# A two-layer hybrid decoder: the second mixer's projection in the 512-column form, with its evacuation, exponentials, transposes and norms re-ordered

## The reference

```python
for i in range(2):
    u = rmsnorm(h, norm_mix_g[i])
    m = rglru_mixer(u, ...) if i == 0 else ssd_mixer(u, ...)
    h = h + m
    h = h + swiglu(rmsnorm(h, norm_ffn_g[i]), ...)
    h = h + sigmoid(rmsnorm(h, norm_ple_g[i]) @ ple_w_gate[i]) * (p[i] @ ple_w_proj[i])
return rmsnorm(h, final_norm_g)

def ssd_mixer(u, ...):
    z, xbc, dt = split(u @ w_in)              # 4096, 6144 and 64 columns
    xbc = silu(causal_dwconv(xbc, conv_w, conv_b))
    x, B, C = split(xbc)                      # 64 heads of 64; 8 groups x state 128
    # chunks of 128 tokens: scores = (C B^T) * exp(segsum(A dt)); y = scores @ (x dt) + state terms
    y = ssd_scan(x, softplus(dt + dt_bias), -exp(a_log), B, C) + d_skip * x
    y = y * silu(z)
    y = y * rsqrt(mean(y*y over each group of 512) + eps) * norm_g
    return y @ w_out
```

## Time and profile before

| | |
|---|---|
| time, median of 3 runs | 2684.93 us (2684.62 to 2686.05) |
| the profiled execution's own time | 2686.58 us |
| its span, first to last instruction | 2684.9 us |
| mean granted PE clock | 0.998 |
| PE, DVE, ACT, POOL busy | 99%, 74%, 52%, 11% of the span |
| loads | 498.88 MB read, 187 GB/s over the span |

### The profile page before, as it was taken

The page is one execution under the profiler, slowest core; times in us unless marked ns, Lnnn a source line. Parts: engine busy times, 40 slices in busy tenths (PEclk is TensorE's granted clock), DMA queues, the critical chain, the costliest instruction groups (busy, mean ns, idle before and its releaser), DMA issues.

```text
span 2684.9 us, 47929 instructions
## 1 busy us (share of the span) xinstructions
PE 2660.2 (99%) x16895; PEld 2399.2 (89%) x16895; DVE 1993.9 (74%) x2782; ACT 1394.8 (52%) x1924; POOL 282.4 (11%) x314
## 2 busy tenths in 40 slices
PE   8999999999999999999999999999999999999998
PEld 8999888888888888899998999988888888888887
DVE  7788776665666678888896788978666556667776
ACT  6776444444444445556764567644444444444454
POOL 1001300000000111100001000032000000001211
PEclk9999999999999999999999999999999999999999
DMA  6545555556655566555555555555555665555564
GB/s 217 180 169 191 180 196 189 190 173 188 204 190 190 194 189 198 188 175 189 182 187 187 197 181 184 188 186 189 191 189 173 188 204 191 189 189 175 188 202 138
DMA packets 157054, 502.54 MB, mean 187 GB/s; under 512 B 16848, under 2 KB 25360, under 8 KB 156816
## 3 DMA queue, kind: packets, MB, share of 16 engines
q1 hardware_dynamic: 156864, 501.04, 57.3%
q10 hardware_dynamic: 80, 0.07, 0.0%
HBM read 498.88 MB, written 2.16 MB: 187 GB/s over the span
## 4 chain that ended last, share of the span: by engine, by line
PE 89%; DVE 5%; ACT 3%; issue 1%; DMA 1%; SPq 0%; DVEq 0%; ACTq 0%
PE bank L408 51%; PE bank L410 26%; PE bank L390 4%; PE bank L392 4%; PE bank L391 4%; DVE wlo L904 2%; ACT whi L615 1%; DMA wraw<-in_A 1%; DVE arena L1114 1%; PE bank L576 0%; ACT L691 0%; DVE R L1005 0%; ACT arena L691 0%; ACT arena L700 0%; PE bank L580 0%
## 5 line engine op out<-in xcount | busy, mean ns | idle before, releaser
L408 PE MATMUL bank<-R,whi 128*128 128x512 f32 x5984 | 2084.9, 393 | 0.2 <-DVE wlo L904 0.2
L410 PE MATMUL bank<-R,wlo 128*128 128x256 f32 x5984 | 1674.1, 280 | 0.0
L904 DVE TENSOR_TENSOR wlo<-wraw,whi 128x1024 fp32r<-128x1024 f32 (+2 forms) x1008 | 1164.0, 1161 | 560.2 <-ACT whi L615 558.9
L615 ACT ACTIVATE whi<-wraw 128x1024 fp32r<-128x1024 f32 (+2 forms) x1008 | 984.1, 983 | 891.4 <-PE bank L410 794.1
L408 PEld LDWEIGHTS bank<-R,whi 128*128 128x128 f32 x5984 | 1120.4, 187 | 251.6 <-DVE wlo L904 0.6
L410 PEld LDWEIGHTS bank<-R,wlo 128*128 128x128 f32 x5984 | 1130.0, 189 | 0.1
L390 PE MATMUL bank<-R,whi 128*128 128x256 f32 x1376 | 392.9, 286 | 6.4 <-DVE wlo L904 5.3
L392 PE MATMUL bank<-R,wlo 128*128 128x256 f32 x1376 | 389.6, 283 | 0.0
L391 PE MATMUL bank<-R,whi 128*128 128x256 f32 x1376 | 389.3, 283 | 0.0
L390 PEld LDWEIGHTS bank<-R,whi 128*128 128x128 f32 x1376 | 262.4, 191 | 10.9 <-DVE wlo L904 6.7
L391 PEld LDWEIGHTS bank<-R,whi 128*128 128x128 f32 x1376 | 262.5, 191 | 0.2
(11 more groups left out here) (173 smaller groups left out, 1314.9 us busy)
## 6 DMA issues: line engine op xcount, KB each, us to landing
wraw<-in_F SPq DMA_DIRECT2D x352, 512.0 KB, 3.3
wraw<-in_B SPq DMA_DIRECT2D x224, 512.0 KB, 3.3
wraw<-in_A SPq DMA_DIRECT2D x96, 512.0 KB, 3.6
wraw<-in_F SPq DMA_DIRECT2D x128, 384.0 KB, 3.1
wraw<-in_F SPq DMA_DIRECT2D x128, 320.0 KB, 3.2
wraw<-in_PL SPq DMA_DIRECT2D x64, 512.0 KB, 3.7
arena<-cs_rows SPq DMA_DIRECT2D x8, 1024.0 KB, 6.4
arena<-in_gates SPq DMA_DIRECT2D x8, 512.0 KB, 3.7
```

The lines of the kernel that those rows point to most:

```text
L408: nc.tensor.matmul(dst.rearrange("p (s t) -> p s t", s=2), whi[:, q % RING, cols], src[:, :, k, :], start=first, stop=False)
L410: mm = nc.tensor.matmul(dst[:, 0:SEQ], wlo[:, q % RING, cols], src[:, 0, k, :], start=False, stop=last)
L615: nc.scalar.activation(whi[:, slot, 0:w * BLOCK], wraw[:, slot, 0:w * BLOCK], ACT.Copy).then_inc(w_hi, 1)
L904: V.tensor_tensor(wlo[:, slot, 0:w * BLOCK], wraw[:, slot, 0:w * BLOCK], whi[:, slot, 0:w * BLOCK].bitcast(F32), ALU.subtract).then_inc(w_ ...
```

## The change

- B1 joins `WIDE`: pieces 0 to 11 take the 512-column form too, so all ten tiles of a group lie in two halves of a bank.
- ACT copies each bank's low half (columns 256 to 511) into `low_half`, in the odd slot of its tile, once PE is done with the tile; DVE adds bank and copy instead of the summing instruction, and then multiplies with 1/rms. The last tap of the tile before stands between the two; a tile's SiLU stands between two taps of the next.
- The decays are made one head a slot, in slots 8 to 15 (in the very first group from slot 11 on, two in slot 17). The transposes come after piece 15, the masks and x in slot 16, the scores in slots 17 and 18.
- Norms take the root first: ACT reads the sum out of the bank, with the mean and epsilon in the instruction, and DVE takes the reciprocal behind it. For a group the root is in slot 5 and the reciprocal in slot 7, ahead of the norm.
- At the end ACT loads the root's table early; DVE copies 1/rms into a bank and multiplies 12 tiles, POOL the other 4.

```diff
-WIDE = ("A2", "F1", "F2", "B2")
-LAST = ((0, 4), (4, 4), (8, 4), (12, 2), (14, 2))
+WIDE = ("A2", "B1", "F1", "F2", "B2")
+LAST = ((0, 3), (3, 3), (6, 3), (9, 2), (11, 1))
+LAST_POOL = ((12, 2), (14, 2))
...
-                            if q == 14:
+                            if q == 15:
                                 pe.wait_ge(silu_done, group * 6 + 6)
...
             def norm(k):
-                act.wait_ge(var_done, k + 1)
-                nc.scalar.activation(rinv[:], rinvh[:], ACT.Sqrt).then_inc(rinv_done, 1)
+                act.wait_ge(stats_done, k + 1)
+                nc.scalar.activation(rinvh[:], bank[6][:, 0:SEQ], ACT.Sqrt, bias=eps[:, 0:1], scale=1.0 / D
+                                     ).then_inc(root_done, 1)
...
+                            if q % 2 == 1:
+                                act.wait_ge(w_used, p + 1)
+                                act.wait_ge(bank_free, it * 10 + ph["group0"] + 4 + q // 2 - 1)
+                                nc.scalar.activation(low_half[:, q // 2 % 2, :], bank[BANKS4[q // 2 % 4]][:, SEQ:2 * SEQ],
+                                                     ACT.Copy).then_inc(half_done, 1)
...
-                            if q == 6 and not first:
-                                group_rinv(group - 1)
+                            if q == 5 and not first:
+                                group_root(group - 1)
...
+                def decays_at(q, very_first):
+
+                    if very_first:
+                        return {17: (6, 7)}.get(q, (q - 11,) if 11 <= q < 17 else ())
+                    return (q - 8,) if 8 <= q < 16 else ()
...
+                                tile = q // 2
+                                dst = cpad[:, tile % 2, 3:3 + SEQ] if tile < 6 else zt[:, tile - 6, :]
+                                dve.wait_ge(half_done, group * 10 + tile + 1)
...
+                                folded = own.mark(V.tensor_tensor(dst, bank[BANKS4[tile % 4]][:, 0:SEQ], low_half[:, tile % 2, :],
+                                                                  ALU.add))
+                                if 1 <= tile <= 6:
+                                    own.need(third)
+                                    last_tap(group, tile - 1)
+                                own.need(folded)
+                                V.tensor_tensor(dst, dst, rinv[:] if tile < 6 else rinvh[:], ALU.mult).then_inc(bank_free, 1)
...
-                            if q in (15, 17):
-                                h0 = 0 if q == 15 else 4
-                                dve.wait_ge(exp_done, group * 4 + h0 // 2 + 2)
+                            if q in (17, 18):
+                                h0 = 0 if q == 17 else 4
+                                dve.wait_ge(exp_done, group * 8 + h0 + 4)
...
                 def group_norm(group):
-                    dve.wait_ge(grinv_done, group + 1)
+                    dve.wait_ge(groot_done, group + 1)
+                    own.link(V.reciprocal(grms[:], grms[:]))
```

More of the change, by code:

```diff
@@ L852, in body @@
                                 z_tanh(it, q - 1, group)
-                            if q in (11, 13, 15, 17):
-                                if q == 11:
+                            for head in decays_at(q, very_first):
+                                if head == 0:
                                     if very_first:
@@ L954, in norm @@
             def norm(k):
-                dve.wait_ge(stats_done, k + 1)
-                own.link(V.tensor_scalar(rinvh[:], bank[6][:, 0:SEQ], 1.0 / D, EPS, ALU.mult, ALU.add))
-                V.reciprocal(rinvh[:], rinvh[:]).then_inc(var_done, 1)
-                dve.wait_ge(rinv_done, k + 1)
-                if k == 6:
-                    return
+                dve.wait_ge(root_done, k + 1)
+                own.link(V.reciprocal(rinv[:], rinvh[:]))
                 own.link(V.tensor_scalar(rinvh[:], rinv[:], 0.5, None, ALU.mult))
@@ L1153, in body @@
                         w = width_of(index, ph, q, last)
+                        if name == "B1" and q == 14:
+                            conv_silu(it + ph["half"] * 4, 5)
                         if w and not (first and index == 0 and q == 0):
@@ L1284, in body @@
                                 group_y(group - 1)
-                            if q == 5 and not first:
-                                group_var(group - 1)
                             if q == 7 and not first:
@@ L1301, in body @@
[L1301 to L1312 removed]
+                                second = tap(group, nt, 2)
@@ L1358, in group_y @@
                         V.tensor_tensor(zt[:, j, :], ca[:, 2 + j, :], zt[:, j, :], ALU.mult).then_inc(yz_done, 1)
-                def group_var(group):
-                    dve.wait_ge(gstat_mm, group + 1)
-                    own.link(V.tensor_scalar(grms[:], bank[7][:, 0:SEQ], 1.0 / 512, EPS, ALU.mult, ALU.add))
-                    V.reciprocal(grms[:], grms[:]).then_inc(gvar_done, 1)
                 def group_norm(group):
-                    dve.wait_ge(grinv_done, group + 1)
+                    dve.wait_ge(groot_done, group + 1)
+                    own.link(V.reciprocal(grms[:], grms[:]))
                     for j in range(4):
@@ L1374, in _ @@
             V.tensor_tensor(swi_u[:, 0, :], h[:, KT - 1, :], h[:, KT - 1, :], ALU.mult).then_inc(last_square, 1)
-            norm(6)
+            dve.wait_ge(root_done, 7)
+            V.reciprocal(rinv[:], rinvh[:]).then_inc(rinv_last, 1)
+            dve.wait_ge(rinv_last, 1)
+            own.link(V.tensor_copy(bank[7][:, 0:SEQ], rinv[:]))
             dve.wait_ge(gained, KT)
```

112 lines of the change are left out of this document (62 added, 50 removed).

## The result

| | before | after |
|---|---|---|
| time, median | 2684.62 us (2684.46 to 2686.05, 5 runs) | 2748.09 us (2745.99 to 2749.14, 5 runs) |
| ratio to before | | 1.0233, 95% interval 1.0221 to 1.0244 |
| span of the profiled run | 2684.9 us | 2746.4 us |
| second mixer's projection, both halves (B1) | 503.7 us | 566.5 us |

The change makes the kernel 2.3% slower. The prediction said 2735 us in a range of 2692 to 2765: right in sign and in kind, 13 us short in size.

The account below looks back on a forecast made before the run. PE, 99% busy, was taken to bound the kernel. To the 2684.93 us median: -9.4 PE's gain, +46.3 and +6.1 waits, -1.6 edges, +9.3 clock, +50.7 in all: 2735 us, range 2692 to 2765 (the forecast's own 2712 to 2757).

Parts of the forecast that it names:

- PE's gain, -9.4: B1's 768 blocks go from three matmuls to two: 10.2 us saved, taken as 9.4 for slower starts after y products.
- Waits, 46.3 + 6.1 = 52.4: PE's waits in B1: 7.7 us in each of six ordinary groups, 46.3; the halves' two first groups together 6.1.
- What makes SiLU 5 late: Root and reciprocal delays from slot 5 on, plus heads, make PE wait 2.0 us at an ordinary group's transposes.
- Series from tanh 5: From ScalarE's tanh of conv tile 5 to the second scores' end: 18.3 us, so PE waits 4.8 at the y products.
- The clock, +9.3: PE drops to 1.2 GHz after long waits, slowing y products by up to 3.1 us; half that price for six waits.
- the bound of 25 us: Upper bound of the clock's cost: all eight groups' y products wholly at half clock, 8 x 3.1 us.
- The other gap rule: The skill's columns/2.4 + 2.5 ns per matmul would save only 1.9 us in all; the trace's 13 ns was preferred.
- Edges, -1.6: The first norm's earlier root saves 0.8 us, and the kernel's end, with products shared with GpSimd, saves 0.8.
- 4 of 16 tiles move to GpSimd: 1.2 us less: At the kernel's end VectorE sheds four tiles at 0.29 us each, against 0.4 for a copy into a bank.
- the backlog never reaches PE: Rival: ScalarE and VectorE keep up with PE in B1, so no waits; -11, 2674 us, chance 0.16.
- The named point of decision: Test of the no-wait rival: second scores starting earlier than 1.75 us ahead of PE's last block of piece 19.
- S8+19: 19 us after PE begins a group's piece 8: the series from tile 5's tanh starting then would avoid the y wait.

Follow-up runs that it names:

- x_oldnorm: The changed kernel with the group norms in the order of before: variance and reciprocal in slot 5, root in slot 6, norms in slot 7; 2732.7 us.
- x_pairs: The changed kernel with the heads' exponentials in pairs in slots 11, 13, 15 and 17, as before; 2745.5 us.
- x_late: x_best2 with masks in slot 16 and scores in slots 17 and 18, as in the changed kernel; 2722.7 us.
- x_warm2: The changed kernel with 18 filler matmuls (12 in each half's first group) on PE ahead of its wait for the second scores; 2730.6 us.
- x_best2: The changed kernel with old group-norm order, old tap and SiLU order, paired heads from slot 9, masks in slot 15, scores mostly in 15 and 16; 2679.9 us.
- x_earlyturn: The changed kernel with transposes and masks in slot 14 and scores in slots 15 and 17, as before; 2731.6 us.
- x_wide: The kernel before with only B1 put in the 512-column form, its banks folded by VectorE's reduction; 2707.1 us.
- x_edges: The kernel before with only root-first whole-row norms, four end tiles on GpSimd and the copy of 1/rms in a bank; 2686.1 us.

## Why the prediction was right, and where it was off

- **PE's gain, -9.4.** The price per block holds: pieces 6 to 9 are 2.77 us long where they were 2.88. Over a group's first ten pieces it is 1.0 us where the faster of two paces (last section) runs throughout, 0.5 to 0.8 in three groups, 7.3 in all eight; with pieces 10 and 11 at 0.11 each some 9.0.
- **Waits, 46.3 + 6.1 = 52.4.** Recorded 47.7: at the transposes about 1.6 in each ordinary group (2.0 predicted), at the y products 4.3 (4.8), for low halves 0.8 (0.9), some 40 where 46.3 was predicted. Of the two first groups one waits 2.8 us (3.2); the very first waits 4.2 (2.9) and 0.8 more at the transposes, where none was predicted. Another 5 us lie in pieces 10 to 14, which are longer than their recorded waits say. Together 53: the term holds, but that it is met to 1 us is partly luck, as waits that were put too high are made up by time that wasn't foreseen.
- **What makes SiLU 5 late.** The prediction led the 2.0 us at the transposes back to the root and the reciprocal, through slots 5 to 9. x_oldnorm takes these away, and 8.7 of 10.4 us stay: their delay goes into pieces 10 to 14. x_pairs shows the heads to be most of it. So here the wait was right, and one of the two causes given for it wrong.
- **Series from tanh 5.** In the third group tanh 5 starts at S8+24.6 (predicted 24.1) and the second scores end 18.2 us behind it (18.3). The series was right; the backlog behind which it was put was not needed. x_late has the same wait without it.
- **The clock, +9.3: the mis-sized term.** It measured 17.5 us (x_warm2), 18.5 in the trace, and that is 8 to 9 of the 13 us by which the forecast was short. I took half of the price for six waits and nothing for the two first groups. The slow clock came after all eight, the one of 2.8 us too, at some 2.2 us each, where half of the clock for all of the y products would have cost 3.1. The Trainium skill (TensorE: Matmul & The Clock Gate, section Why this matters for your kernels) names idle gaps between bursts as what drops the clock. By it all six ordinary groups fall, and the bound of 25 us is nearer than 0. The traces agree with both: against my half this was the better guide, though the whole price was not paid.
- **The other gap rule.** I had set the Trainium skill's formula (the same page, section Back-to-back issue gap) against the row, with a gain of 1.9 us. That section gives the formula for a single isolated matmul, and says that in a stream of weight loads and matmuls both set the spacing. This kernel is such a stream, so the formula was no rival; the pieces show the row's 13 ns a block, as predicted.
- **Edges, -1.6.** The first norm gave about 1.8 us in the changed kernel (0.8 predicted; 0.8 to 2.4 over the kernels with the same first stage) and the end nothing (0.8), because the step "4 of 16 tiles move to GpSimd: 1.2 us less" stopped at VectorE and didn't follow SP's seven stores.
- **Rivals.** That the backlog never reaches PE was out of this change's reach, but not of the form's: x_best2 is that rival made true (2680; I had 2674). The named point of decision, that the second scores start 1.75 us before PE's last block of piece 19, is met there: they end at 1339.0, and PE is through piece 19 at 1339.8. Its other condition, that it would do for the series to start at S8+19, forgot that PE comes sooner too when nothing holds it at the transposes: in x_late it starts at S8+20.3, and the wait is 4.2 us all the same.
- **The range.** The forecast's own range of 2712 to 2757 has a lower end that its terms don't give: 2726 less 6 is 2720.

The sum with measured terms, against the spans: -9.0 + 47.7 + 5 + 18.5 = 62.2 of the 62.7 us in B1. With -1.8 in the first stage and +0.6 ahead of PE's first weight product the spans differ by 61.5.

## What to carry to other kernels

When PE is the bound, a stall costs its own length and the slow clock behind it: here 4.3 us of wait cost up to 7.1. So price a long wait with its clock, and don't count on a short one being spared (next section); a few matmuls in the idle time tell the two costs apart. A product that PE needs at a fixed place should be followed back through its series on the other engines, and be placed by its end; one or two slots of position made 43 us, while the faster form itself was worth 9. And follow the end of a kernel to its last store: fewer products with more stores is no gain.

## What the runs showed of the hardware

- **How long a wait may be.** PE was busy at 1.00 ahead of all these waits of B1. Behind waits of up to 1.7 us the granted clock stayed at 1.00, and behind every one of 3.4 us or more (changed kernel, x_oldnorm, x_earlyturn, x_pairs, x_late) it was 0.50 for a while. Between them it went either way: ten waits were 2.0 to 2.8 us long, and seven were followed by 0.50, the shortest 2.0 (x_wide), while one of 2.8 was not. The price isn't fixed by the wait either: in the changed kernel the y products lost from 1.4 to 2.8 us after waits of 4.1 to 4.3.
- **Two paces of one form.** The 512-column form runs a piece of eight blocks in 2.77 or in 2.83 us, for long stretches, at the same clock. ScalarE's splits, which wait for PE, show it in the first layer's output stage, x_edges first and then the kernel before, the code of that stage being the same:

```profile
256.56 1.06 ACT L623 ACTIVATE whi<-wraw 128x1024 fp32r<-128x1024 f32 x1 [1.26 <-PE bank L418]
...
259.33 1.06 ACT L623 ACTIVATE whi<-wraw 128x1024 fp32r<-128x1024 f32 x1 [0.87 <-PE bank L418]
```

```profile
259.06 1.06 ACT L615 ACTIVATE whi<-wraw 128x1024 fp32r<-128x1024 f32 x1 [1.37 <-PE bank L410]
...
261.88 1.06 ACT L615 ACTIVATE whi<-wraw 128x1024 fp32r<-128x1024 f32 x1 [1.24 <-PE bank L410]
```

  The stage takes 89.35 us in the one and 90.97 in the other. In B1 it is x_edges that has the slower pace, 1.8 us in all. In the traces the pace changes only where PE has been held up or has done other products in between; what sets it isn't shown. It moves a time by 1 to 2 us, so here a forecast of less than that could not be told from it.
- **GpSimd beside VectorE.** While GpSimd writes its low parts of the normed tiles, a VectorE product over 256 columns takes 0.95 us in place of 0.42 and a low half 1.76 in place of 1.22 (rows of the changed kernel above). GpSimd's four:

```profile
1327.38 4.47 POOL L1470 TENSOR_TENSOR R<-arena,R 128x256 f32 x4 [16.70 <-ACT R L906]
```

  It goes both ways: they take 1.03, 0.91, 0.92 and, beside the low half, 1.71 us. VectorE's addition in the same stretch, which has one of its inputs in a bank, takes its usual 0.42. In the kernel before, too, a low half took 1.43 us beside them. They come right behind the norms, with ScalarE's high parts.
